# 128 gathered tokens in place of 96 beside the dense experts of a PEER layer, with VectorE alone splitting the second phase's weights

## The chip, the cores and the metric

One core of one Trainium2 chip. The metric is the device time of the whole program in microseconds (us): 3645.8 us is the median of three runs of the kernel before (3645.3 to 3651.99).

## The reference

Two transformer layers, a hybrid mixer and a cross-attention come first; the change does not touch them. It lies in the last layer, PEER: each of 512 tokens chooses 8 x 16 = 128 of 16384 experts by product keys, and the result is a gated sum over them.

```
q = (t @ wq).reshape(ntok, 8, 2, 128)
sc = einsum('thpd,hpkd->thpk', q, subkeys)
s1, i1 = top_k(sc[:, :, 0], 16); s2, i2 = top_k(sc[:, :, 1], 16)
cand = (s1[..., :, None] + s2[..., None, :]).reshape(ntok, 8, 256)
best, pos = top_k(cand, 16)
idx = i1[pos // 16] * 128 + i2[pos % 16]
gate = softmax(best)
act = gelu(einsum('phkd,pd->phk', u_tab[idx], tb)) * gate
out = einsum('phk,phkd->pd', act, v_tab[idx])
```

## The kernel before, in words

**Dense part.** Most tokens are not gathered: for them all 16384 experts are computed. The experts are 128 tiles of 128. In the first phase (steps i = 0 to 127, `up`, L3099) TensorE multiplies the u tile by 416 tokens, ScalarE applies gelu (L3230) and stores the tile to DRAM (`store`, L3202). In the second phase (L3154) the activations come back, are multiplied by gates that are zero for the experts a token did not choose (`gated`, L3450), and are multiplied by the v tile into eight accumulators in PSUM.

**Weights in two parts.** To keep fp32 precision each weight tile is split: SyncE loads it to RAW (L266, three buffers), ScalarE copies it rounded to fp32r (L275), VectorE subtracts the rounded part from the tile (L284, four buffers of both parts), and TensorE makes three matmuls for each of 8 slices (L317 to L319; L3160 to L3162), 24 in a step. For tiles 5 to 67 of the first phase POOL does half of the subtraction (L290; `self.pooled`). ScalarE and VectorE work two or three tiles ahead of TensorE.

**Choice.** Scores (L3102) and top-16 lists (`choice`, L3327) are made on VectorE, for four blocks of 128 tokens in the order 3, 0, 1, 2, in 38 pieces each that are dealt out over the steps (`pieces_by`, L2993). ScalarE makes the exponentials (L3244); `share` (L3370) divides.

**Gates.** From step 70 on a gate tile is built for 8 tokens in each step: one-hot rows of the first index times the gate (L3387) and of the second index (L3390 on VectorE for the first four tokens, L3506 on POOL for the others), multiplied on TensorE (L3136). ScalarE evicts 128x1024 values (L3213) into one of two halves of a buffer; after 64 tokens (a fill) the half is written to DRAM (L3071, L3262). There are seven fills, one of 32 tokens (steps 70 to 73) and six of 64 (from step 74, eight steps each). In the second phase each step reads a gate tile of 416 tokens (L3065).

**Gathered part.** The other 96 tokens (rows 32 to 127 of block 3, 64 and 32 of them) are laid out so that 96 gathers of 128 rows of u serve them: POOL issues an indirect DMA for one row in each partition (L3494), VectorE takes the product and its sum (`dot`, L3408). 46 dots stand at steps 21 to 66 with five buffers, 50 at 77 to 126 with three. In the second phase 96 gathers of v rows with eight buffers, and `sum_` (L3416) adds the scaled rows.

**Order.** Each engine follows one program, written by hand. An engine stops at a wait and everything behind it on that engine stops too. On VectorE a step is: subtraction for tile i + 2, dots, pieces of the choice, one-hots; in the second phase: subtraction, gated, remainder (`rest`, L3455), sums. On ScalarE: weight copy for tile i + 3, gelu, store, evictions, writes of gates.

Of the kernel before, what the change touches and what calls it, by code (L numbers as in the profile page):

```python
# [86 lines left out]
def program(nc, A, out, known, seen):  # L87
# [5 lines left out]
    with ctx:  # L93
# [41 lines left out]
        Gd = nc.dram_tensor("gates_dram", (128, 128, 416), F, kind="Internal").ap()  # L135
        Ad = nc.dram_tensor("acts_dram", (128, 128, 416), F, kind="Internal").ap()
# [16 lines left out]
        g_last = [sem(f"g_last{i}") for i in range(8)]  # L153
        few_in = sem("few_in")
# [22 lines left out]
        T2 = 512  # L177
# [2767 lines left out]
        TD, FEW, HALVES = 416, 96, 64  # L2945
        xtm, few_ = qb(place(1024), 1024), qb(place(192), 192)
        few_i = qb(place(64), 64).bitcast(U32)
        few3 = few_.rearrange("p (i s) -> p i s", i=3)
        spare = UF[:, 0:16 * T2].rearrange("p (k c) -> p k c", c=T2)
        xtm4, four3 = spare[:, :, 416:480], spare[:, 0:3, 480:512]  # L2950
        few = [[few_[:, 64 * i:64 * i + 64] for i in range(3)], [spare[:, i, 480:512] for i in range(3)]]
        few_index = [few_i, spare[:, 3, 480:512].bitcast(U32)]
        gu = [qb(oOn, 1024), qb(oOn + 1024, 1024)] + [qb(oGb + 13312 + 1024 * i, 1024) for i in range(3)]
        gu2 = [CH[:, 1024 * i:1024 * i + 1024] for i in range(3)]
        gv_ = [qb(oGb + 1024 * i, 1024) for i in range(8)]
        few_y = [qb(oGb + 8192, 1024), qb(oGb + 13824, 1024)]
# [8 lines left out]
        ggate = [qb(oOn + 2048 + i * 512, 512) for i in range(4)]  # L2965
        Y = [qb(oY + i * 512, 512) for i in range(4)]
        Gb = [MQ[:, oGb + 8192 * i:oGb + 8192 * i + 8192].rearrange("p (n t) -> p n t", t=64) for i in range(2)]
        scs = [qb(oGb + i * 2048, 2048) for i in range(4)]
# [19 lines left out]
        ORDER = [3, 0, 1, 2]  # L2988
        HERE = 46
        FILLS = [(3, 384, 4)] + [(g // 2, 64 * g, 8) for g in range(6)]  # L2990
        FILL_AT = [70] + [74 + 8 * g for g in range(6)]

        def pieces_by(i):  # L2993
            return 38 * i / 14 if i < 14 else 38 + 114 * (i - 14) / 54

        def exp_at(i):
            return [n for c, n in enumerate(ORDER) if i == 18 * c + 15]

        def share_at(i):
            return [n for c, n in enumerate(ORDER) if i == 18 * c + 16]  # L3000

        def turn_at(i):
            return [n for c, n in enumerate(ORDER) if i == 18 * c + 18]

        def dots_at(i):
            return [s_ for s_ in range(FEW) if i == dot_at(s_)]

        def dot_at(s_):
            return 21 + 45 * s_ // (HERE - 1) if s_ < HERE else 77 + 49 * (s_ - HERE) // (FEW - 1 - HERE)

        def rows(s_):

            return (gu[s_ % 5], gu_in[s_ % 5], s_ // 5 + 1) if s_ < HERE else (
                gu2[s_ % 3], gu_in[5 + s_ % 3], (s_ - HERE) // 3 + 1)

        def gathers_at(i):
            return [s_ for s_ in range(FEW) if i == (
                (18 if s_ < 5 else dot_at(s_ - 5) + 1) if s_ < HERE else (75 if s_ < HERE + 3 else dot_at(s_ - 3) + 1))]

        def sums_at(i):  # L3020
            return [s_ for s_ in range(FEW) if i == 6 + 114 * s_ // 95]

        def group(s_):

            return (0, s_) if s_ < HALVES else (1, s_ - HALVES)
# [11 lines left out]
        def out_sp(i):  # L3037
            return [(f, c) for f in range(7) for c in range(8) if i == last_at(f) + 5 + 3 * c // 4]

        def out_act(i):  # L3040
            return [(f, c) for f in range(7) for c in range(8, 16) if i == last_at(f) + 1 + 3 * (c - 8) // 4]

        def half_of(f):
            return (f + 1) % 2

        def gates_out(f, c):
            lo, m = FILLS[f][1], 8 * FILLS[f][2]
            return (Gd[8 * c:8 * c + 8, :, lo:lo + m].rearrange("n p t -> p n t"), Gb[half_of(f)][:, 8 * c:8 * c + 8, 0:m])

        def peer_sp(e):  # L3050
            def back(j):
# [4 lines left out]
                if j == 0:  # L3056
                    e.wait_ge(g_out[0], 16 * 48)
                if j % 8 == 0 and j < 64:
                    e.wait_ge(g_last[j // 8], 16)
                elif j == 64:  # L3060
                    e.wait_ge(g_out[1], 16 * 56)
# [3 lines left out]
                e.dma_start(ggate[j % 4][:, 0:TD], Gd[j]).then_inc(ga_in[j % 4], 16)  # L3065

            for i in range(NB + 4):
                W.sp(e, iU + i)
                for f, c in out_sp(i):
                    e.wait_ge(S.sem, S.at("gates", f, FILLS[f][2] - 1))  # L3070
                    e.dma_start(*gates_out(f, c)).then_inc(g_last[c] if f == 6 else g_out[half_of(f)], 16)  # L3071
# [6 lines left out]
        def peer_pe(e):  # L3078
# [46 lines left out]
            def gates(n, t8):  # L3125
# [54 lines left out]
        def peer_act(e):  # L3180
# [25 lines left out]
            def evict(n, t8):  # L3206
# [8 lines left out]
                ps.give(S, "gates", n, t8)  # L3215

# [6 lines left out]
            for i in range(NB):  # L3223
# [40 lines left out]
            e.wait_ge(V.sem, V.at("dot", FEW - 1))  # L3264
            for a, _, _ in few:
                e.activation(a, a, ACT.Gelu_apprx_tanh).then_inc(S.sem, S.tick("few"))

            for i in range(NB):
                W.act(e, iD + i + 2)
                if i + 1 < NB:  # L3270
                    rounded(i + 1)
            for d in range(8):
# [4 lines left out]
        def peer_dve(e):  # L3277
# [102 lines left out]
            def one_hots(n, t8):  # L3380
                for half in range(2):
                    i4 = four_at(n, t8) + half
                    a, o, t0 = onA[i4 % 4], onB[i4 % 4], FILLS[n][1] + 8 * t8 + 4 * half
                    if i4 >= 4:
                        e.wait_ge(T.sem, T.at("on", i4 - 4))
                    for i in range(4):
                        e.tensor_scalar(a[:, 128 * i:128 * i + 128], iota, E1[:, t0 + i:t0 + i + 1], Gt[:, t0 + i:t0 + i + 1],  # L3387
                                        ALU.is_equal, MUL).then_inc(V.sem, V.tick("onA", i4))
                    if i4 % 2 == 0:
                        e.tensor_tensor(o.rearrange("p (t n) -> p t n", t=4), iota.unsqueeze(1).to_broadcast([128, 4, 128]),  # L3390
                                        E2[:, t0:t0 + 4].unsqueeze(2).to_broadcast([128, 4, 128]), ALU.is_equal).then_inc(
                                            V.sem, V.tick("onA", i4))

            def indices():

                e.wait_ge(V.sem, V.at("chosen", 3))
                three = CH[:, 1152:1536].rearrange("p (i s) -> p i s", i=3)
                e.tensor_copy(few3[64:128], three[64:128, :, 64:128]).then_inc(V.sem, V.tick())
                e.tensor_copy(four3[32:64], three[32:64, :, 32:64]).then_inc(V.sem, V.tick())
                e.wait_ge(few_in, 16 * 8)  # L3400
# [365 lines left out]
```

## Time and profile before

| | us |
|---|---|
| median of 3 runs | 3645.8 |
| the profiled execution | 3639.07 |
| its span, first to last instruction | 3637.2 |
| TensorE busy in it | 3538.1 |
| VectorE, ScalarE, POOL busy | 2284.6, 1472.4, 884.6 |

The first phase lies at 2356 to 3042 us of the span, the second at 3044 to 3622 us. PE is TensorE, PEld its weight loads, DVE VectorE, ACT ScalarE, SP SyncE. A busy share is an average over a stretch; which engine sets the pace is read from who waits for whom. Matmuls overlap, so their duration (some 350 ns) is longer than their distance; the distance is a stretch's time divided by its number of matmuls.

### The profile page before, as it was taken

To read this page: it belongs to the slowest core of one execution; us is meant where nothing else is said; L and a number is where in the kernel's file an instruction comes from. 1 tells how busy PE (TensorE), PEld (TensorE's weight loads), DVE (VectorE), ACT (ScalarE), POOL (GpSimd) and SP (SyncE) were. 2 spreads that over 40 slices of the span, in tenths; PEclk is the share of its full clock that TensorE was granted. 3 is DMA by queue.
4 is the path that set the end of the run, shared out by engine and by line. 5 is a ranking of instruction groups with operands and counts; after the bars stand their busy time and mean duration, and the time that the engine had idled before them with its cause. 6 is when DMAs were issued, how large, how long until landed. Compare 5 with 4: busy or idle time off the path is not lost.

```text
span 3637.2 us, 56094 instructions
## 1 busy us (share of the span) xinstructions
PE 3538.1 (97%) x22572; PEld 3247.0 (89%) x22572; DVE 2284.6 (63%) x3965; ACT 1472.4 (40%) x2191; POOL 884.6 (24%) x795
## 2 busy tenths in 40 slices
PE   8999999999899999999998999999999999999998
PEld 8988999999797678788677877899999999999998
DVE  7445465554844545555687444479988885777775
ACT  7254453222625435222466444243333433333333
POOL 4010022111401012211213201035646662111110
PEclk9999999999999999999999999999999999999999
DMA  4212232222221123222222122348869999999894
GB/s 155 70 42 65 76 116 93 93 92 94 70 65 54 63 82 133 95 97 93 75 81 70 60 93 81 95 140 272 281 214 258 298 289 338 314 310 313 307 312 139
DMA packets 293617, 544.70 MB, mean 150 GB/s; under 512 B 138288, under 2 KB 187568, under 8 KB 292976
## 3 DMA queue, kind: packets, MB, share of 16 engines
q1 hardware_dynamic: 185248, 394.34, 32.6%
q0 software_dynamic: 27648, 100.68, 8.4%
q10 hardware_dynamic: 80464, 46.10, 4.3%
q8 instruction: 180, 2.95, 0.3%
q14 instruction: 77, 0.63, 0.0%
HBM read 483.67 MB, written 56.62 MB: 149 GB/s over the span
## 4 chain that ended last, share of the span: by engine, by line
PE 86%; DVE 8%; ACT 3%; issue 1%; POOL 1%; DMA 0%; ACTq 0%; DVEq 0%; POOLq 0%
PE PSM L317 19%; PE PSM L318 18%; PE PSM L319 18%; PE PSM L211 5%; PE PSM L3160 5%; PE PSM L3162 5%; PE PSM L3161 5%; PE PSM L3136 3%; DVE PARTS L284 2%; ACT PARTS L275 1%; PE PSM L1061 1%; DVE MH L1741 1%; PE PSM L825 1%; PE PSM L1097 1%; DVE QK L1375 1%
## 5 line engine op out<-in xcount | busy, mean ns | idle before, releaser
L284 DVE TENSOR_TENSOR PARTS<-RAW,PARTS 128x1024 fp32r<-128x1024 f32 (+1 forms) x612 | 743.8, 1220 | 476.4 <-ACT PARTS L275 476.2
L275 ACT ACTIVATE PARTS<-RAW 128x1024 fp32r<-128x1024 f32 x612 | 645.4, 1057 | 932.1 <-PE PSM L319 488.6
L317 PE MATMUL PSM<-UX,PARTS 128*128 128x264 f32 (+3 forms) x2912 | 987.1, 339 | 27.4 <-DVE UX L2297 4.9
L318 PE MATMUL PSM<-UX,PARTS 128*128 128x264 f32 (+3 forms) x2912 | 970.2, 333 | 0.0
L319 PE MATMUL PSM<-UX,PARTS 128*128 128x264 f32 (+3 forms) x2912 | 969.5, 333 | 0.0
L317 PEld LDWEIGHTS PSM<-UX,PARTS 128*128 128x128 f32 x2912 | 548.8, 188 | 78.4 <-issue 9.2
L318 PEld LDWEIGHTS PSM<-UX,PARTS 128*128 128x128 f32 x2912 | 549.0, 189 | 29.9 <-issue 1.7
L319 PEld LDWEIGHTS PSM<-UX,PARTS 128*128 128x128 f32 x2912 | 547.9, 188 | 29.7
L3160 PE MATMUL PSM<-AC,PARTS 128*128 128x416 f32 x1024 | 358.3, 350 | 2.3 <-DVE AC L3457 2.3
L3162 PE MATMUL PSM<-AC,PARTS 128*128 128x416 f32 x1024 | 357.6, 349 | 0.0
L3161 PE MATMUL PSM<-AC,PARTS 128*128 128x416 f32 x1024 | 357.5, 349 | 0.0
L317 PE MATMUL PSM<-HD,PARTS 128*128 128x264 f32 (+1 forms) x992 | 315.3, 318 | 15.0 <-DVE XL L600 13.1
L319 PE MATMUL PSM<-HD,PARTS 128*128 128x264 f32 (+1 forms) x992 | 314.8, 317 | 0.0
L318 PE MATMUL PSM<-HD,PARTS 128*128 128x264 f32 (+1 forms) x768 | 247.3, 322 | 0.0
L1679 POOL TENSOR_TENSOR FT<-FT 128x528 f32<-128x528 f32 (+1 forms) x56 | 108.3, 1935 | 458.2 <-DVE FT L1708 458.2
L317 PEld LDWEIGHTS PSM<-HD,PARTS 128*128 128x128 f32 x992 | 187.4, 189 | 29.5 <-DVE XL L600 14.1
L319 PEld LDWEIGHTS PSM<-HD,PARTS 128*128 128x128 f32 x992 | 187.3, 189 | 13.2
L3160 PEld LDWEIGHTS PSM<-AC,PARTS 128*128 128x128 f32 x1024 | 192.4, 188 | 2.9 <-ACT MQ L3230 2.6
L3161 PEld LDWEIGHTS PSM<-AC,PARTS 128*128 128x128 f32 x1024 | 192.4, 188 | 0.3
L3162 PEld LDWEIGHTS PSM<-AC,PARTS 128*128 128x128 f32 x1024 | 192.3, 188 | 0.4
L3230 ACT ACTIVATE MQ<-PSM 128x416 f32<-128x416 f32 x128 | 66.1, 517 | 293.6 <-PE PSM L319 293.6
L3506 POOL TENSOR_SCALAR MQ<-MH,MQ 128x128 f32<-128x128 f32 x208 | 171.0, 834 | 52.5 <-PE PSM L3136 28.5
(516 smaller groups left out, 5815.9 us busy)
## 6 DMA issues: line engine op xcount, KB each, us to landing
RAW<-w_ff_dram SPq DMA_DIRECT2D x128, 512.0 KB, 3.2
RAW<-peer_u_dram SPq DMA_DIRECT2D x128, 512.0 KB, 4.8
RAW<-peer_v_dram SPq DMA_DIRECT2D x128, 512.0 KB, 5.1
RAW<-w_in_dram SPq DMA_DIRECT2D x116, 512.0 KB, 3.2
acts_dram<-MQ ACTq DMA_DIRECT2D x128, 208.0 KB, 4.2
MQ<-acts_dram SPq DMA_DIRECT2D x128, 208.0 KB, 3.8
MQ<-gates_dram SPq DMA_DIRECT2D x128, 208.0 KB, 4.7
RAW<-w_mix_o_dram SPq DMA_DIRECT2D x32, 512.0 KB, 3.3
```

The costliest lines, as they stand in the source:

```text
L211: m = e.matmul(PSM[0:rows, b + s, 0:hi - lo], lhs[k], rhs[k][:, lo:hi], start=(k == 0), stop=(k == len(lhs) - 1))
L275: e.activation(p[:, 0:1024], self.raw.of(i), ACT.Copy).then_inc(S.sem, S.tick("w", i))
L284: e.tensor_tensor(p[:, 1024:1024 + n], r[:, 0:n], p[:, 0:n].bitcast(F), SUB).then_inc(V.sem, V.tick("w", i))
L317: e.matmul(dst, wh[k], xh_[k][:, lo:hi], start=(k == 0), stop=False, skip_group_check=True)
L318: e.matmul(dst, wh[k], xl_[k][:, lo:hi], start=False, stop=False, skip_group_check=True)
L319: m = e.matmul(dst, wl[k], xh_[k][:, lo:hi], start=False, stop=(k == kk - 1), skip_group_check=True)
L1679: e.tensor_tensor(x, x, x, MUL).then_inc(G.sem, G.tick("relu2", l, i))
L3136: m = e.matmul(PSM[:, b + half, 128 * i:128 * i + 128], a[:, 128 * i:128 * i + 128], o[:, 128 * i:128 * i + 128], start=True, stop=True, s ...
L3160: e.matmul(PSM[:, acc[d], 0:TD], vh[d], ah, start=(i == 0), stop=False, skip_group_check=True)
L3161: e.matmul(PSM[:, acc[d], 0:TD], vh[d], al, start=False, stop=False, skip_group_check=True)
L3162: m = e.matmul(PSM[:, acc[d], 0:TD], vl[d], ah, start=False, stop=(i == NB - 1), skip_group_check=True)
L3506: e.tensor_scalar(o[:, 128 * i:128 * i + 128], iota, E2[:, t0 + i:t0 + i + 1], None, ALU.is_equal).then_inc(G.sem, G.tick("onB", i4))
```

## The change

384 tokens are computed densely and 128 are gathered, which is all of block 3.

- The 32-token fill goes. The layout of the gathered tokens becomes one token for each partition, so the copies between partitions (eight small DMAs) go.
- 108 dots stay in the first phase: 30 at steps 21 to 70, 78 at steps 80 to 126 with three buffers. The last 20 dots and all 128 sums move to one list of 148 items over steps 6 to 122 of the second phase, with seven buffers in a space that the first phase's tokens held. ScalarE's gelu of the 128 dots moves to step 20 of the second phase.
- The choice ends at steps 15, 34, 53 and 72 (before: all four by step 68), and POOL's half of the subtraction reaches to tile 73. The set `pooled` holds no tile of the second phase, so the two places where the second phase asks for it find nothing: VectorE subtracts there alone, and POOL only issues gathers.
- One-hots of the first index for the second four tokens of a step go from VectorE to ScalarE, as relu(1 - |index - i|) in five instructions; they carry no gate, which POOL's one-hots of the second index now multiply in.
- Fills 0 to 3 go to DRAM in runs of 64 x 8 values, and come back for four steps at a time; fills 4 and 5 stay in SBUF, so `gated` becomes two products of 128 and 256 columns.

```diff
-                self.pooled = {first["pu"] + i for i in range(5, 68)}
+                self.pooled = {first["pu"] + i for i in range(5, 74)}
...
-        TD, FEW, HALVES = 416, 96, 64
+        TD, FEW, LATE = 384, 128, 20
...
+        gv_ = [UF[:, 1024 * i:1024 * i + 1024] for i in range(7)]
...
+        ORDER, END = [3, 0, 1, 2], [15, 34, 53, 72]
+        HERE, THERE = 30, FEW - LATE
+        FILLS = [(g // 2, 64 * g, 8) for g in range(6)]
+        FILL_AT = [74 + 8 * g for g in range(6)]
...
+            return 21 + 50 * s_ // (HERE - 1) if s_ < HERE else 80 + 46 * (s_ - HERE) // (THERE - 1 - HERE)
...
+        def late_by(r):
+            return 6 + 116 * r // (FEW + LATE - 1)
...
+        def late_gathers_at(i):
+            return [r for r in range(FEW + LATE) if i == (0 if r < 7 else late_by(r - 7) + 1)]
...
+            return Gd[f, :, 8 * c:8 * c + 8, :], Gb[half_of(f)][:, 8 * c:8 * c + 8, :]
...
+                if j % 4 == 0:
+                    if j >= 8:
+                        e.wait_ge(V.sem, V.at("gated", j - 5))
+                    e.dma_start(ggate[j // 4 % 2].rearrange("p (f m) -> p f m", f=4),
+                                Gd[:, :, j:j + 4, :].rearrange("f p n t -> p f (n t)")).then_inc(gg_in[j // 4 % 2], 16)
...
+            def one_hots(n, t8):
+                i4 = four_at(n, t8) + 1
+                a, t0 = onA[i4 % 4], FILLS[n][1] + 8 * t8 + 4
...
+                for i in range(4):
+                    e.activation(a[:, 128 * i:128 * i + 128], iota, ACT.Abs, bias=E1[:, t0 + i:t0 + i + 1],
+                                 scale=-1.0).then_inc(S.sem, S.tick("off", i4))
+                e.wait_ge(S.sem, S.at("off", i4))
+                e.activation(a, a, ACT.Relu, bias=con["ones"][:, 0:1], scale=-1.0).then_inc(S.sem, S.tick("onA", i4))
...
+                for n, t8 in gates_at(i + 1):
+                    one_hots(n, t8)
                 for n, t8 in gates_at(i):
                     evict(n, t8)
...
+                e.tensor_tensor(y, y, kept[:, i], MUL).then_inc(V.sem, V.tick())
+                e.wait_ge(gg_in[i // 4 % 2], 16 * (i // 8 + 1))
+                e.tensor_tensor(x, x, gate4[i // 4 % 2][:, i % 4], MUL).then_inc(V.sem, V.tick("gated", i))
...
-                    e.tensor_scalar(o[:, 128 * i:128 * i + 128], iota, E2[:, t0 + i:t0 + i + 1], None,
-                                    ALU.is_equal).then_inc(G.sem, G.tick("onB", i4))
+                    e.tensor_scalar(o[:, 128 * i:128 * i + 128], iota, E2[:, t0 + i:t0 + i + 1], Gt[:, t0 + i:t0 + i + 1],
+                                    ALU.is_equal, MUL).then_inc(G.sem, G.tick("onB", i4))
...
+            for i in range(NB):
+                if iD + i + 2 in W.pooled:
+                    W.pool(e, iD + i + 2)
+                for r in late_gathers_at(i):
+                    if r == 0:
+                        e.wait_ge(T.sem, T.at("pu", NB - 1))
+                    if r >= LATE + 7:
+                        e.wait_ge(V.sem, V.at("sum", r - LATE - 7))
+                    elif r >= 7:
+                        e.wait_ge(V.sem, V.at("dot", THERE + r - 7))
```

## Rows read from the trace of the kernel before

**Rows 1.** The page, part 1: busy us (share of the span) xinstructions.

```profile
PE 3538.1 (97%) x22572; PEld 3247.0 (89%) x22572; DVE 2284.6 (63%) x3965; ACT 1472.4 (40%) x2191; POOL 884.6 (24%) x795
```

**Rows 2.** Stretches: us, busy PE, PEld, DVE, ACT, POOL; clock; DMA share; GB/s.

```profile
600.00:900.00 300.00, 300.00 (x2476) 300.00 (x2475) 150.53 (x155) 72.91 (x83) 54.69 (x29) 1.00 0.28 92
1500.00:1750.00 250.00, 250.00 (x1085) 203.76 (x1084) 131.82 (x138) 61.65 (x68) 43.66 (x23) 1.00 0.29 95
...
2460.00:2690.00 230.00, 230.00 (x1225) 228.56 (x1225) 227.09 (x731) 84.56 (x111) 124.55 (x93) 1.00 0.80 270
2700.00:3010.00 310.00, 310.00 (x1984) 309.92 (x1983) 252.72 (x586) 125.05 (x151) 210.03 (x244) 1.00 0.95 274
3030.00:3060.00 30.00, 27.74 (x141) 27.24 (x140) 14.04 (x21) 9.80 (x16) 3.49 (x3) 0.94 1.12 359
3060.00:3100.00 40.00, 40.00 (x216) 39.94 (x215) 27.88 (x35) 13.52 (x19) 13.48 (x10) 1.00 1.02 398
3100.00:3600.00 500.00, 500.00 (x2681) 499.22 (x2680) 356.49 (x426) 168.03 (x224) 77.77 (x83) 1.00 0.87 298
```

**Rows 3.** Waits at 3100 to 3600 us: total, times, longest.

```profile
ACT PARTS L275 <- PE PSM L3162: 333.7, 112, 3.0
```

**Rows 4.** The chain of waits, two gate steps: start, us, what.

```profile
2750.19 1.78 PE PSM L3136 x16
2756.45 1.78 PE PSM L3136 x16
```

**Rows 5.** Waits at 3020 to 3060 us.

```profile
DVE MQ L3453 <- DMA MQ<-gates_dram: 3.7, 3, 2.1
...
PE PSM L3160 <- DVE AC L3457: 2.3, 1, 2.3
```

**Rows 6.** VectorE's groups at 2460 to 2690 us, the dots: xcount | busy, mean ns.

```profile
L3413 DVE SCALAR_TENSOR_TENSOR MQ<-MQ 128x1024 f32<-128x1024 f32 x46 | 55.9, 1216 | 0.0
...
L3413 DVE DVE_READ_ACCUMULATOR MQ<-MQ 128x1 f32 x46 | 3.7, 81 | 0.0
```

**Rows 7.** Groups at 2700 to 3010 us, the gate stage.

```profile
L3506 POOL TENSOR_SCALAR MQ<-MH,MQ 128x128 f32<-128x128 f32 x196 | 159.0, 822 | 29.0 <-PE PSM L3136 28.5
...
L3387 DVE TENSOR_SCALAR MQ<-MH,MQ 128x128 f32<-128x128 f32 x397 | 116.5, 353 | 0.0
...
L275 ACT ACTIVATE PARTS<-RAW 128x1024 fp32r<-128x1024 f32 x50 | 52.6, 1052 | 8.2 <-ACT MQ L3213 4.3 <-issue 3.6
L3213 ACT ACTIVATE MQ<-PSM 128x1024 f32<-128x1024 f32 x50 | 51.2, 1025 | 65.6 <-PE PSM L3136 59.5 <-DVE MQ L3387 2.5 <-issue 2.3
```

**Rows 8.** ScalarE's groups at 2380 to 3640 us.

```profile
L3244 ACT ACT_TABLE_LOAD x4 | 5.1, 1283 | 0.1
...
L3244 ACT ACTIVATE CH<-CH 128x128 f32<-128x128 f32 x4 | 1.2, 311 | 0.4 <-DVE CH L3367 0.4
```

**Rows 9.** ScalarE's queue and POOL in order of time, 2770 to 2784 us.

```profile
2781.56 0.34 ACTq L3204 DMA_DIRECT2D acts_dram<-MQ  x1
...
2770.94 2.60 POOL L3506 TENSOR_SCALAR MQ<-MH,MQ 128x128 f32<-128x128 f32 x4 [0.60 <-PE PSM L3136]
...
2777.21 4.64 POOL L3506 TENSOR_SCALAR MQ<-MH,MQ 128x128 f32<-128x128 f32 x4 [0.32 <-PE PSM L3136]
```

**Rows 10.** The gathers of the gate stage, by groups and by line L3494.

```profile
L3494 POOL DMA_INDIRECT CH<-peer_rows_dram,UF x30 | 31.5, 1049 | 46.9 <-DVE MQ L3387 46.9
...
DMA to landing us min/median/max: 4.3/6.3/9.3
```

**Rows 11.** DMA packets at 2700 to 3010 us.

```profile
DMA packets 121046, 84.98 MB, mean 274 GB/s; under 512 B 102192, under 2 KB 108592, under 8 KB 121020
```

**Rows 12.** VectorE's groups at 3100 to 3600 us, the second phase.

```profile
L284 DVE TENSOR_TENSOR PARTS<-RAW,PARTS 128x1024 fp32r<-128x1024 f32 x112 | 137.2, 1225 | 143.5 <-ACT PARTS L275 143.5
L3429 DVE SCALAR_TENSOR_TENSOR MQ<-MQ 128x1024 f32<-128x1024 f32 x59 | 75.5, 1280 | 0.0
L3453 DVE TENSOR_TENSOR MQ<-MQ 128x416 f32<-128x416 f32 x112 | 65.4, 584 | 0.0
```

More of the change, by code:

```diff
@@ L2944, in program @@
         sm = qb(place(16), 16)
[L2945 to L2952 removed]
+        TD, FEW, LATE = 384, 128, 20
+        xtm = qb(place(1024), 1024)
+        few_a, few_g, few_i = qb(oE1 + TD, 128), qb(oGt + TD, 128), qb(oE2 + TD, 128).bitcast(U32)
         gu = [qb(oOn, 1024), qb(oOn + 1024, 1024)] + [qb(oGb + 13312 + 1024 * i, 1024) for i in range(3)]
         gu2 = [CH[:, 1024 * i:1024 * i + 1024] for i in range(3)]
[L2955 to L2956 removed]
+        gv_ = [UF[:, 1024 * i:1024 * i + 1024] for i in range(7)]
+        few_y = UF[:, 7168:8192]
         assert at[0] <= STAGE - 3072
@@ L2980, in program @@
         iP, iU, iD = first["pq"], first["pu"], first["pd"]
[L2988 to L2991, printed above, removed]
+        ORDER, END = [3, 0, 1, 2], [15, 34, 53, 72]
+        HERE, THERE = 30, FEW - LATE
+        FILLS = [(g // 2, 64 * g, 8) for g in range(6)]
+        FILL_AT = [74 + 8 * g for g in range(6)]
         def pieces_by(i):
-            return 38 * i / 14 if i < 14 else 38 + 114 * (i - 14) / 54
+            c = sum(i >= x for x in END)
+            if c == 4:
+                return 38 * 4
+            lo = END[c - 1] if c else 1
+            return 38 * c + 38 * (i - lo) / (END[c] - lo)
@@ L3016, in gathers_at @@
-        def gathers_at(i):
[L3017 to L3025, printed above, removed]
+            if s_ < HERE:
+                return gu[s_ % 5], gu_in[s_ % 5], s_ // 5 + 1
+            return gu2[s_ % 3], gu_in[5 + s_ % 3], (s_ - HERE) // 3 + 1
@@ new lines, in late, with late_at @@
+        def late(r):
+            return gv_[r % 7], gv_in[r % 7], r // 7 + 1
+        def gathers_at(i):
+            return [s_ for s_ in range(THERE) if i == (
+                (18 if s_ < 5 else dot_at(s_ - 5) + 1) if s_ < HERE else (77 if s_ < HERE + 3 else dot_at(s_ - 3) + 1))]
+        def late_by(r):
+            return 6 + 116 * r // (FEW + LATE - 1)
+        WHOLE = late_by(LATE)
+        def late_at(i):
+            return [r for r in range(FEW + LATE) if i == late_by(r)]
+        def late_gathers_at(i):
+            return [r for r in range(FEW + LATE) if i == (0 if r < 7 else late_by(r - 7) + 1)]
@@ L3056, in back @@
                 if j == 0:
[L3057 to L3061, printed above, removed]
+                    for out_ in g_out:
+                        e.wait_ge(out_, 16 * 32)
                 if j >= 4:
@@ L3271, in peer_act @@
                     rounded(i + 1)
+                if i == WHOLE - 1:
+                    e.wait_ge(V.sem, V.at("dot", FEW - 1))
+                    e.activation(few_a, few_a, ACT.Gelu_apprx_tanh).then_inc(S.sem, S.tick("few"))
             for d in range(8):
@@ L3380, in one_hots @@
             def one_hots(n, t8):
[L3381 to L3392, printed above, removed]
+                i4 = four_at(n, t8)
@@ L3408, in dot @@
             def dot(s_):
-                x, landed, turn_ = rows(s_)
-                w, c = group(s_)
+                x, landed, turn_ = rows(s_) if s_ < THERE else late(s_ - THERE)
                 e.wait_ge(landed, 16 * turn_)
-                xv = x.rearrange("p (k c) -> p k c", c=64) if w else x
-                e.scalar_tensor_tensor(out=xv, in0=xv, scalar=1.0, in1=xtm4 if w else xtm, op0=MUL, op1=MUL,
-                                       accum_out=few[w][0][:, c:c + 1]).then_inc(V.sem, V.tick("dot", s_))
+                if s_ == 0:
+                    e.wait_ge(S.sem, S.at("xtm"))
@@ L3416, in sum_ @@
+                e.scalar_tensor_tensor(out=x, in0=x, scalar=1.0, in1=xtm, op0=MUL, op1=MUL,
+                                       accum_out=few_a[:, s_:s_ + 1]).then_inc(V.sem, V.tick("dot", s_))
             def sum_(s_):
-                w, c = group(s_)
-                x, a, y = gv_[s_ % 8], few[w][0][:, c:c + 1], few_y[w]
-                e.wait_ge(gv_in[s_ % 8], 16 * (s_ // 8 + 1))
+                x, landed, turn_ = late(LATE + s_)
+                a = few_a[:, s_:s_ + 1]
+                e.wait_ge(landed, 16 * turn_)
@@ L3528, in peer_pool @@
                     one_hots(n, t8)
-            e.wait_ge(g_out[0], 16 * 48)
-            for s_ in range(FEW):
-                if s_ >= 8:
-                    e.wait_ge(V.sem, V.at("sum", s_ - 8))
-                else:
-                    e.wait_ge(V.sem, V.at("al", s_ + 1))
-                gather(gv_[s_ % 8], A["peer_v"].rearrange("n p d -> (n p) d"), s_, gv_in[s_ % 8])
+            for i in range(NB):
[8 more added lines that the diff above has]
+                        e.wait_ge(V.sem, V.at("dot", THERE + r - 7))
+                    to, landed, _ = late(r)
+                    if r < LATE:
+                        gather(to, A["peer_rows"], THERE + r, landed)
+                    else:
+                        gather(to, A["peer_v"].rearrange("n p d -> (n p) d"), r - LATE, landed)
             for p in range(3):
```

121 lines of the change are left out of this document (53 added, 68 removed).

## The prediction

> **What bounds the kernel now.** I read the page first: PE is busy 3538.1 of 3637.2 us [rows 1]. A matmul's busy time overlaps its neighbours', so I went to the table of stretches next and counted matmuls per us. In the second phase (3100 to 3600 us) 2681 matmuls of 416 columns take 500 us, 186.5 ns each, and weight loads fill 499.22 us [rows 2]: PE runs back to back. The waits of that stretch say the same from the other side: ACT waited 112 times, 2.98 us each, for PE to hand a weight buffer back [rows 3]. VectorE is busy 356.49 of 500 us, the DMA engines 0.87 [rows 2]. In the first phase PE is busy for all of the choice (2460 to 2690) and all of the gate stretch (2700 to 3010), with VectorE at 227.09 of 230 and 252.72 of 310 [rows 2]. The chain of waits shows a gate step: two gate products start 6.26 us apart and take 1.78 [rows 4], which leaves 4.48 for the 24 weight matmuls. So TensorE sets the pace of all 256 steps, and the change must be judged by the columns that it takes away and by whether anything else can keep the shorter step.
>
> **Columns.** Dense tokens go from 416 to 384, in 2 x 128 x 24 = 6144 matmuls. No row has 384 columns. The rows beside it: 264 columns 300/2476 = 121.2 ns, 416 columns 186.5, 512 columns 250/1085 = 230.4 [rows 2]. Between 264 and 416 a column costs 0.430 ns, between 416 and 512 0.457; 32 columns are 13.75 to 14.6 ns. I take 13.75, since 384 lies in the first interval: **-84.5 us** (bound -89.8). A step becomes 24 x 172.7 ns = 4.15 us, a gate step 4.15 + 1.78 = 5.93.
>
> **Gate steps.** The fill of 32 tokens at steps 70 to 73 goes; 48 gate steps stay of 52. Four times 1.78 us [rows 4]: **-7.1 us**.
>
> **Between the phases.** PE waited 2.3 us once for the first gated activations, and these for a gate tile's DMA, 3.7 us in all [rows 5], because the last fill was written to DRAM and read back. Now fills 4 and 5 stay in SBUF and the first gate quad can be read long before. PE still waits for the last gelu (0.5 us): **-2 us**; bounds 0, if something else is late there, and -4, as the granted clock was only 0.94 in 3030 to 3060 and may not fall [rows 2]. The constants before the first gather, eight small transfers and their waits, go too; PE did not wait for them, so nothing.
>
> **Choice stage.** Dots here fall from 46 to 30, each 1.216 + 0.081 us [rows 6], 20.8 us of VectorE's work, and the choice is spread over 4 more steps. VectorE's 227 us become 206 plus 3 for four more weight halves, in 51 steps x 4.15 + 16.6 = 228 us: 92%. Cover is there, and it is thinner only at the three 2048-element operations that end each block. Nothing, bound +6.
>
> **Gate stage, engine by engine, against 5.93 us.**
> VectorE loses four of its eight one-hot products (353 ns each, [rows 7]) and gains dots: 78 dots in 47 steps, 1.66 a step. Now 252.72/49.5 steps = 5.1 us; minus 4 x 0.27 (that is 353 less the overlap) plus 0.66 x 1.30 gives 4.9.
> ACT takes the four products over: four Abs of 128x128, for which the nearest row is an exponential of 128x128, 311 ns [rows 8], and a Relu of 512 columns, which I put between 0.52 and 0.65 us (below a 1024-column eviction's 1.025, [rows 7]). With the copy of the weights 1.05 and the eviction 1.03 [rows 7], a gelu of 384 columns between the two (0.5) and 1.67 transfers to issue at 0.34 [rows 9] this is 1.9 + 3.2 = 5.1 us. The one-hots stand ahead of the eviction on ACT, and the next weight copy behind it, so VectorE's step starts about 1 us later than now. No row shows Abs. If it needed a table of its own, two loads of 1.283 us [rows 8] would come to each gate step: ACT at 7.7, 1.8 us over, 48 x 1.8 = +86. The Trainium skill (ScalarE: Activation LUTs, Table sets: the hidden batching unit) says that relu and abs are in every set; no run here shows it, and without that sentence I would still hold it unlikely, since copies and gelus alternate here without a load.
> POOL multiplies the gate into its one-hots: the same four instructions with a second operation. Now 0.822 us each [rows 7], four of them between 2.60 and 4.64 us [rows 9]. With 1.66 gathers of 1.049 [rows 10] POOL is at 3.3 + 1.7 = 5.0 us. The price of the second operation is not in the trace: from nothing to a doubling (1.64 us). I take 0 to 0.2, since the long and the short times of one and the same instruction show that most of it is not arithmetic.
> DMA: gates are written in 2 KB runs for four fills in place of 256 B runs for seven; under 512 B were 102192 of 121046 packets in this stage [rows 11]. Per step 0.52 MB of weights, 0.87 of gathers, 0.20 of activations, 0.52 of gates: 2.1 MB in 5.93 us, 357 GB/s, against 274 now at a share of 0.95 [rows 2].
> What is tight is the **gather loop**: three buffers, 1.66 dots a step. In one step out of three a gather is issued in the step of its own dot: dot, POOL's issue, landing (4.3, median 6.3, at most 9.3 us, [rows 10]), dot, one-hots, PE. From the dot that frees the buffer to PE's need of the one-hots there are about 5.93 + 4.1 = 10 us; 6.3 + 1.3 + 1.7 = 9.3 fits, 9.3 + 3.0 = 12.3 does not. Some 16 such steps, I charge 0.6 us each: **+10 us** (0 to 37).
>
> **Second phase against 4.15 us.** VectorE alone subtracts the rounded weights, as it does now: no item of this kernel's second phase moves to or from POOL. What grows is the sums: 148 dots and sums in 117 steps, 1.265 each. From 584 ns for 416 columns and 1225 for 1024 [rows 12] a column is 1.054 ns and the fixed part 146: the two gated products of 128 and 256 columns 0.28 + 0.42, the remainder of 384 columns 0.55. Sum 1.225 + 0.70 + 0.55 + 1.265 x 1.28 = 4.09 us without any overlap. A step now is by the same rows 1.225 + 2 x 0.584 + 0.83 x 1.28 = 3.46 us, where the stretch has VectorE busy for 356.49 us in 2681/24 = 111.7 steps, 3.19 each [rows 2]: instructions overlap to 0.92, so 3.77 us. It holds, with 9% to spare, and two buffers' lead (weights are split two steps ahead) evens out steps with two sums. If a gather lands late, the next subtraction is queued behind the sum that waits for it; with seven buffers a gather has some 4.5 steps, 18 us, for a landing of 5 to 9.
> DMA per step: 0.524 weights, 1.265 x 0.524 gathers, 0.197 activations, 0.131 gates: 1.515 MB, 365 GB/s, against 298 now. The highest sustained row is 398 GB/s at 3060 to 3100, with PE at its full rate (216 matmuls in 40 us, [rows 2]). So it fits, at 92%. **0 us** (to +33).
> The Trainium skill (DMA: Bandwidth & Descriptors, Specifications) gives about 358 GB/s of HBM for one core; by it the step is estimated at 4.23 us and this phase 10 us longer. The 398 of the row is above that figure, and the row decides.
>
> **Sum.** -84.5 - 7.1 - 2 + 10 = -84; a further stall of about 1 us where the gates begin (exponential, share and the first one-hots in one step) is as it is now. The profiled execution's 3639.1 (span 3637.2) becomes 3555; it lies 6.7 below the median of 3645.8, to which I apply the same difference: **3562 us**. VectorE, POOL and ACT only lose cover; what becomes late next is the gather loop in the gate stage.
>
> **Rivals.**
> A, the gather loop bounds the gate stage: three dots per 1.3 + 3.3 (POOL in its one-hots) + 6.3 + 1.1 = 12 us means 6.65 us a step, +0.72 x 47 = 34 in place of 10: 3586. For it: landing times to 9.3 and POOL busy in order. Against: DMA's small packets vanish. Chance 0.16.
> B, the second phase becomes DMA-bound: 1.515 MB at 359 GB/s (row 3030 to 3060, share 1.12) is 4.22 us, at 298/0.87 = 343 GB/s 4.42; 117 steps x 0.07 to 0.27 = +8 to +32: 3570 to 3594. Against: the 398 row. Chance 0.13. The Trainium skill's 358 GB/s, above, would land in this case.
> C, nothing stalls: 3552 or, with 14.6 ns, 3547. Chance 0.14, part of the forecast's neighbourhood.
> D, slower: POOL's one-hots with two operations cost twice, 1.64 us. Then POOL needs 4 x 1.64 + 1.7 = 8.3 us in each of 48 gate steps, PE waits 2.4, +114: 3552 + 114 = 3666. It decides from 1.54 us an instruction, where 48 steps of 4 x 1.54 + 1.74 give the 94 us back. For it: collisions already bring four to 4.64 us. Chance 0.07. With ACT's table loads (3638) 0.02.
> E, VectorE is over the second phase's step because chained sums cannot overlap: 4.3 us, +18: 3580. Chance 0.05.
> That the change does not do what it says: POOL's weights end at step 73 of the first phase, so it can't take one in the second; no chance given.
>
> **How the numbers follow.** The forecast with small stalls has 0.43. The range holds C, the forecast, A and B's most: 3545 to 3598; D and the sum of A and B are left out. A measurement of this kernel tells some 0.2%, 7 us: faster 0.91, same 0.02 (table loads and a mild D), slower 0.07 (D).
>
> **What would show it.** Right: second phase with 172 to 174 ns between matmuls and PE without idle time, VectorE near 3.8 us a step, DMA near 365 GB/s; gate steps 5.93 with a few longer, whose wait is on VectorE behind a gather. Wrong: PE waiting on POOL's one-hots (D), on ACT's, or in the second phase on VectorE while that waits for a gather (B) or for nothing (E).

## The result and the profile after

The changed kernel takes 3630.7 us at the median (3647.6 before, on the same chips): ratio 0.9947, 95% interval 0.9935 to 0.9959. It is faster, by 0.5% where 2.3% were forecast; 3562 us missed by 69, and the range ended at 3598. The profiled execution took 3626.0 us, span 3624.2. Two disturbed executions, of 6894 us here and of 4817 us in the run without dots below, count in no median.

The table of stretches (us, busy PE, PEld, DVE, ACT, POOL; clock; DMA share; GB/s), which answers to [rows 2]:

```profile
3100.00:3600.00 500.00, 500.00 (x2886) 500.00 (x2886) 441.54 (x647) 176.03 (x240) 189.56 (x141) 1.00 0.95 348
2460.00:2690.00 230.00, 225.68 (x1304) 224.74 (x1303) 225.44 (x695) 92.57 (x126) 119.38 (x81) 1.00 0.72 235
2700.00:3010.00 310.00, 260.99 (x1620) 254.75 (x1619) 196.64 (x366) 175.27 (x324) 278.57 (x224) 0.94 0.77 256
```

The second phase is as forecast: 500/2886 = 173.3 ns from one matmul to the next, PE without a gap. The loss is all in the third line. PE is busy for 261 of 310 us and POOL for 279, where it was 210 [rows 2]. From the starts of the weight matmuls, steps 78 to 120 of the first phase are 7.58 us apart on the mean, with single ones up to 13.4; 5.93 were forecast, and 6.27 were measured before. From the start of step 78 to that of step 120 are 42 such distances: 42 x 1.65 = 69 us, as much as the miss.

The line numbers below are those of the changed kernel: L3511 is POOL's one-hots (before: L3506), L3499 its gathers (L3494), L3420 the dots (L3413), L3400 and L3402 VectorE's one-hots of the first and of the second index (L3387, L3390), L283 its subtraction (L284), L3147 the gate products (L3136). In the experiments they shift by some lines.

The groups of that stage, 2720 to 3000 us, as in [rows 7, 10] (xcount | busy, mean ns of one | idle time before):

```profile
L3511 POOL TENSOR_SCALAR MQ<-MH,MQ 128x128 f32<-128x128 f32 x146 | 179.1, 1233 | 2.8 <-PE PSM L3147 1.4
L3499 POOL DMA_INDIRECT CH<-peer_rows_dram,MQ x59 | 77.4, 1312 | 21.8 <-DVE MQ L3400 11.0 <-issue 7.9 <-DVE CH L3420 1.6
...
L3420 DVE SCALAR_TENSOR_TENSOR CH<-CH,MQ 128x1024 f32<-128x1024 f32 x60 | 74.0, 1242 | 69.8 <-DMA CH<-peer_rows_dram,MQ 69.6
L3400 DVE TENSOR_SCALAR MQ<-MH,MQ 128x128 f32<-128x128 f32 x140 | 47.1, 420 | 0.0
L283 DVE TENSOR_TENSOR PARTS<-RAW,PARTS 128x1024 fp32r<-128x1024 f32 x36 | 44.5, 1236 | 25.8 <-ACT PARTS L274 25.8
```

and the waits there (total, times, longest):

```profile
DVE CH L3420 <- DMA CH<-peer_rows_dram,MQ: 69.6, 25, 7.0
...
PE PSM L3147 <- DVE MQ L3402: 28.0, 11, 5.6
PE PSM L3147 <- POOL MQ L3511: 10.0, 7, 2.5
```

POOL's one-hot takes 1.23 us in place of 0.82, its gather 1.31 in place of 1.05. Yet the longest waits name VectorE, behind a dot that waits for a landing. Read by those rows alone, the gather loop would be the cause.

PE's waits there come to 43 of 280 us, but the stage has lost 60: 280 us hold 37 steps, each 1.63 us over the undisturbed 5.95. The other 17 us are time in which PE is busy longer for the same matmuls. The granted clock is 0.95 on the mean from 2720 to 3000 us, where it was 1.00 before, and 280 us at 0.95 lack 14 us of full clock. It fell after PE had stood (columns as in [rows 2]):

```profile
2885.00:2890.00 5.00, 1.36 (x8) 1.04 (x6) 1.08 (x1) 2.38 (x6) 2.70 (x4) 0.90 0.97 344
2890.00:2895.00 5.00, 3.06 (x14) 3.08 (x15) 5.00 (x13) 0.00 (x0) 4.53 (x3) 0.50 0.69 190
```

0.50 is the lower of the two levels, 1.2 in place of 2.4 GHz. So a wait of PE cost more here than its own length.

The order of time shows why POOL's instruction is long. POOL first, then VectorE (start, us, what):

```profile
2849.66 6.24 POOL L3511 TENSOR_SCALAR MQ<-MH,MQ 128x128 f32<-128x128 f32 x4
...
2859.38 3.13 POOL L3511 TENSOR_SCALAR MQ<-MH,MQ 128x128 f32<-128x128 f32 x4
```

```profile
2848.95 1.53 DVE L283 TENSOR_TENSOR PARTS<-RAW,PARTS 128x1024 fp32r<-128x1024 f32 x1 [1.98 <-ACT PARTS L274]
2850.40 1.21 DVE L3420 SCALAR_TENSOR_TENSOR CH<-CH,MQ 128x1024 f32<-128x1024 f32 x1
2851.54 0.08 DVE L3420 DVE_READ_ACCUMULATOR CH<-CH,MQ 128x1 f32 x1
2851.54 1.22 DVE L3420 SCALAR_TENSOR_TENSOR CH<-CH,MQ 128x1024 f32<-128x1024 f32 x1
2852.69 0.08 DVE L3420 DVE_READ_ACCUMULATOR CH<-CH,MQ 128x1 f32 x1
2852.69 1.16 DVE L3400 TENSOR_SCALAR MQ<-MH,MQ 128x128 f32<-128x128 f32 x4
2853.77 0.68 DVE L3402 TENSOR_TENSOR MQ<-MH,MQ 128x512 f32<-128x512 f32 x1
...
2863.59 1.23 DVE L3420 SCALAR_TENSOR_TENSOR CH<-CH,MQ 128x1024 f32<-128x1024 f32 x1 [5.23 <-DMA CH<-peer_rows_dram,MQ]
```

At 2859.38 VectorE waits for a landing, and four one-hots take 3.13 us, 0.78 each. At 2849.66 VectorE is in a run of three instructions without a gap that each read two tensors from SBUF; the run ends at 2852.77. The first of POOL's four, by itself:

```profile
2849.66 3.61 POOL L3511 TENSOR_SCALAR MQ<-MH,MQ 128x128 f32<-128x128 f32 x1
```

It takes 2.8 us more than one alone and ends 0.5 us after the run: POOL stood until the run was over. VectorE's one-hots after it (L3400, one tensor) cost POOL's second 0.07 us (0.86), the comparison L3402 (two tensors) its third 0.22 (1.01). Of the 46 one-hots of POOL at 2720 to 3000 us that started with more than 0.4 us of such a run left, 42 ended 0.50 to 0.68 us after its end; four ended before it. All of POOL's one-hots there, sorted by what VectorE did meanwhile (an overlap of over 10 ns counts):

```
POOL's one-hots, mean ns (count)     before (1 operation)   after (2 operations)
VectorE idle                          600 (34)               792 (57)
only one-tensor instructions beside   658 (78)               none
a two-tensor instruction beside      1130 (68)              1517 (88)
```

The Trainium skill (SBUF — State Buffer, Who interferes with whom) has this as a rule: a VectorE instruction with two SBUF inputs and a GpSimd (POOL) instruction that reads SBUF use the same port, and the one that starts later is blocked until the other ends. The rows agree that one blocks the other. They show that POOL mostly stood not only for the instruction that was running when it came, but for the run of them. That the resource is a port is the page's statement; the runs show the blocking.

### The profile page after: what moved, and what is told of

It reads as the page before. It is cut to its first block, busy times and chain, and to the rows that moved or that the text cites. A ratio compares the mean times of both kernels' runs of the same rounds, so it can differ in the third digit from the quotient of the medians.

```text
span 3624.2 us, 56046 instructions
## 1 busy us (share of the span) xinstructions
PE 3468.8 (96%) x22489; PEld 3173.6 (88%) x22489; DVE 2311.8 (64%) x3955; ACT 1548.5 (43%) x2424; POOL 1096.1 (30%) x849
## 4 chain that ended last, share of the span: by engine, by line
PE 77%; DVE 10%; POOL 5%; ACT 3%; DMA 3%; issue 2%; ACTq 0%; DVEq 0%; POOLq 0%
PE PSM L316 17%; PE PSM L317 16%; PE PSM L318 16%; PE PSM L210 5%; PE PSM L3173 5%; PE PSM L3174 5%; PE PSM L3175 5%; POOL MQ L3511 3%; DMA CH<-peer_rows_dram,MQ 3%; DVE PARTS L283 2%; ACT PARTS L274 1%; POOL CH L3499 1%; DVE CH L3420 1%; PE PSM L1060 1%; DVE MH L1740 1%
## 5 line engine op out<-in xcount | busy, mean ns | idle before, releaser
L316 PE MATMUL PSM<-UX,PARTS 128*128 128x264 f32 (+3 forms) x2912 | 978.0, 336 | 29.5 <-DVE UX L2296 4.9
L283 DVE TENSOR_TENSOR PARTS<-RAW,PARTS 128x1024 fp32r<-128x1024 f32 (+1 forms) x612 | 743.5, 1220 | 358.4 <-ACT PARTS L274 358.1
L317 PE MATMUL PSM<-UX,PARTS 128*128 128x264 f32 (+3 forms) x2912 | 960.3, 330 | 0.0
L318 PE MATMUL PSM<-UX,PARTS 128*128 128x264 f32 (+3 forms) x2912 | 959.3, 329 | 0.0
L3173 PE MATMUL PSM<-AC,PARTS 128*128 128x384 f32 x1024 | 343.0, 335 | 0.9 <-ACT MQ L3248 0.9
L3174 PE MATMUL PSM<-AC,PARTS 128*128 128x384 f32 x1024 | 342.4, 334 | 0.0
L3175 PE MATMUL PSM<-AC,PARTS 128*128 128x384 f32 x1024 | 342.3, 334 | 0.0
L3499 POOL DMA_INDIRECT UF<-peer_v_dram,MQ x128 | 174.8, 1366 | 245.4 <-DVE UF L3432 217.0
L3511 POOL TENSOR_SCALAR MQ<-MH,MQ 128x128 f32<-128x128 f32 x192 | 231.7, 1213 | 17.6 <-DVE CH L3381 14.5
```

Of the source, the lines that this page charges most:

```text
L283: e.tensor_tensor(p[:, 1024:1024 + n], r[:, 0:n], p[:, 0:n].bitcast(F), SUB).then_inc(V.sem, V.tick("w", i))
L316: e.matmul(dst, wh[k], xh_[k][:, lo:hi], start=(k == 0), stop=False, skip_group_check=True)
L317: e.matmul(dst, wh[k], xl_[k][:, lo:hi], start=False, stop=False, skip_group_check=True)
L318: m = e.matmul(dst, wl[k], xh_[k][:, lo:hi], start=False, stop=(k == kk - 1), skip_group_check=True)
L3173: e.matmul(PSM[:, acc[d], 0:TD], vh[d], ah, start=(i == 0), stop=False, skip_group_check=True)
L3174: e.matmul(PSM[:, acc[d], 0:TD], vh[d], al, start=False, stop=False, skip_group_check=True)
```

## The experiments

Time is a kernel's median, the ratio is to the kernel before; "steps" is the mean distance of steps 78 to 120, read as above. Edits are shortened to what matters. Two theories stood first: POOL's own work bounds the gate stage, or the loop of three gather buffers does.

**POOL compares only.**

```diff
-  e.tensor_scalar(o[...], iota, E2[...], Gt[...], ALU.is_equal, MUL)
+  e.tensor_scalar(o[...], iota, E2[...], None, ALU.is_equal)
```

> POOL's one-hots of the gate stage go back to one operation (the comparison alone); the gates of the second four tokens of each step are left out. The changed kernel takes 3631 us and its 48 gate steps average 7.5 us where 5.93 were forecast. Theory 1 (POOL is the bound: four one-hots at 1.22 us and 1.7 gathers at 1.34 fill its step): with 0.82 us an instruction POOL needs 3.3 + 2.3 = 5.6 us, gate steps fall to 6.0 to 6.4 and the time to 3565 to 3585. Theory 2 (the loop of three gather buffers, dot to issue to landing to dot, is the bound): the loop loses only the 1.6 us that POOL's one-hots are shorter in the steps where a gather is issued behind them, steps stay at 7.0 to 7.4, time 3610 to 3625.

3593.6 us, ratio 0.9847 (0.9830 to 0.9865), steps 6.76: 37 us faster than the changed kernel, half of what was missing. Theory 2's range is left by far, theory 1's missed by 9 us: its 0.82 us for one comparison did not hold either, as the group shows.

```profile
L3511 POOL TENSOR_SCALAR MQ<-MH,MQ 128x128 f32<-128x128 f32 x163 | 158.6, 985 | 3.1 <-PE PSM L3147 1.8
```

**No gathers.**

```diff
+  if s_ >= HERE + 3: continue        # POOL's gathers of the gate stage
-  e.wait_ge(landed, 16 * turn_)      # the dot
+  e.wait_ge(V.sem, V.at("dot", s_ - 3))
```

> The 75 gathers of the gate stage from the fourth on are left out, and with them the waits of the dots for their landing; the 75 dots still run, on rows that are not theirs. Theory 1: POOL has only its one-hots, 4 x 1.22 = 4.9 us, below 5.93, so steps fall to 5.93 to 6.1 and the time to 3555 to 3568. Theory 2: the loop is gone, the same 3555 to 3568. A third theory (VectorE beside it stretches POOL's four one-hots to some 6 us whether it gathers or not): steps stay at 6.2 to 6.6, time 3573 to 3592.

3557.2 us, 0.9752 (0.9736 to 0.9768), steps 5.95. So nothing but POOL, its gathers and their transfers stands between the changed kernel and the forecast; the first two theories had the same range and are not told apart. The third theory fell on the time, but its mechanism is in the group: with VectorE never stopped for a landing, a one-hot of POOL takes 1.47 us, and four fill 5.9 of a 5.95 us step.

```profile
L3514 POOL TENSOR_SCALAR MQ<-MH,MQ 128x128 f32<-128x128 f32 x173 | 252.8, 1474 | 2.7 <-PE PSM L3147 2.7
```

**No dots.** VectorE's 78 dots of the gate stage are left out; a gather waits for the landing of the third before it.

```diff
-  dot(s_)
+  if s_ < HERE: dot(s_)
-  e.wait_ge(V.sem, V.at("dot", s_ - 3))                      # POOL, before a gather
+  e.wait_ge(rows(s_ - 3)[1], 16 * rows(s_ - 3)[2])
```

> The gathers of the gate stage stay, but its 78 dots are left out; each gather waits only for the landing of the one three before it. Theory 1 (POOL's own work): POOL still has 4 x 1.22 + 1.7 x 1.34 = 7.2 us of work in a step, steps 6.8 to 7.4, time 3600 to 3627. Theory 2 (the loop): no dot and no late landing stands ahead of VectorE's one-hots, steps 5.93 to 6.1, time 3555 to 3568. In between (6.2 to 6.7, 3573 to 3597) if POOL's instructions are 1.22 us only because VectorE works beside them: VectorE loses 1.7 x 1.24 = 2.1 us of each step.

3574.7 us, 0.9805 (0.9785 to 0.9824), steps 6.43: the middle case. POOL has as many instructions in a step as in the changed kernel, but its one-hots are shorter, with VectorE busy for 128.9 of 280 us in place of 179.3.

```profile
L3514 POOL TENSOR_SCALAR MQ<-MH,MQ 128x128 f32<-128x128 f32 x168 | 177.1, 1061 | 3.0 <-PE PSM L3147 1.4
```

**POOL in the second phase.**

```diff
-  self.pooled = {first["pu"] + i for i in range(5, 74)}
+  self.pooled = {first["pu"] + i for i in range(5, 74)} | {first["pd"] + i for i in range(8, 120)}
```

> The second phase's remainders of the weights are halved between VectorE and POOL, as in the first phase; the rest is the changed kernel. The forecast's own step (the second phase is TensorE's at 4.16 us, VectorE at 3.67 has room): no change, 3624 to 3638. A rival (VectorE is near its limit there and saves time with half of the subtraction gone): would be faster by up to 10 us, but PE shows no idle time to win. The other rival (POOL, with 1.37 us gathers and four subtractions of some 0.9 us each, delays gathers or VectorE): slower, 3640 to 3670.

3666.1 us, 1.0059 (1.0040 to 1.0078): 35 us slower than the changed kernel, as the other rival said; with POOL's half, the whole change would be no gain. The kernel before leaves this work to VectorE as well, so here the change keeps something; it is no source of its gain. PE is busy for 469.5 of 500 us at 3100 to 3600, where the changed kernel has it busy for all. Groups of VectorE at 3100 to 3500 us:

```profile
L3432 DVE SCALAR_TENSOR_TENSOR UF<-UF,MQ 128x1024 f32<-128x1024 f32 x92 | 165.7, 1802 | 2.0
L283 DVE TENSOR_TENSOR PARTS<-RAW,PARTS 128x512 fp32r<-128x512 f32 x89 | 73.8, 829 | 1.3 <-ACT PARTS L274 1.3
L3464 DVE TENSOR_TENSOR AC<-MQ,AC 128x384 fp32r<-128x384 f32 x88 | 70.1, 796 | 0.0
L3458 DVE TENSOR_TENSOR MQ<-MQ 128x128 f32<-128x128 f32 x89 | 59.9, 673 | 0.3 <-DMA MQ<-acts_dram 0.3
```

In the changed kernel the same sums take 1.281 us, the remainders 0.553 and the products of 128 columns 0.285. POOL takes 512 columns off a 1.22 us instruction, and what VectorE saves, some 0.4 us, it pays back with some 1.1 us in longer instructions: here POOL holds up VectorE.

**The gate on ScalarE**, all outputs kept, POOL comparing only:

```diff
-  e.activation(a, a, ACT.Relu, bias=ones, scale=-1.0)
+  for i in range(4):
+      e.activation(x_i, x_i, ACT.Relu, bias=Gt[...], scale=NG[...])     # NG = -Gt
...
-  e.tensor_scalar(o[...], iota, E2[...], Gt[...], ALU.is_equal, MUL)    # POOL
+  e.tensor_scalar(o[...], iota, E2[...], None, ALU.is_equal)
```

> The gate of the second four tokens moves from POOL's one-hots to ScalarE's: Relu with scale -gate and bias gate, four of 128 columns in place of one of 512, and POOL compares only. Nothing is left out. ScalarE had 3.85 us of work in a 5.95 us step where no gather stood in the way, and gets some 0.85 more. Theory 1 (POOL's own work, lengthened while VectorE works): as with the comparison alone, 3588 to 3600. If ScalarE's later one-hots became the wait: 3605 to 3630.

3593.2 us, 0.9856 (0.9840 to 0.9873), steps 6.81, as theory 1 said. ScalarE had the room: busy for 215.7 of 280 us.

**Wide one-hots on POOL.**

```diff
-  4 x e.tensor_scalar(o_i, iota, E2[...], None, ALU.is_equal)
+  e.tensor_tensor(o4, iota4, E2 broadcast, SUB); e.tensor_scalar(o, o, 0.0, None, ALU.is_equal)
```

> As the run before it (gate on ScalarE), and POOL makes its four one-hots in two instructions of 512 columns (a subtraction of the token's number, a comparison with zero) in place of four of 128. Theory 1: POOL has 1.3 to 1.6 us for the subtraction, about 1.2 for the comparison, and 1.7 gathers of 1.4: 5.0 us, some 1.2 less than with four comparisons; steps 6.0 to 6.3, time 3565 to 3582. Theory 2 (three gather buffers bound what is left): 3585 to 3597. A rival: a two-input subtraction on POOL lengthens VectorE's instructions, as in the second phase where POOL subtracted; then VectorE is late, 3595 to 3620.

3594.9 us, 0.9864 (0.9848 to 0.9881), steps 6.83: no gain over four comparisons. The time lies where theory 2 and the rival's lower end meet, and VectorE's groups speak for the rival: dots of 1.56 us in place of 1.25. But POOL's comparison also took 2.13 us where about 1.2 were expected, so the run does not tell the two apart.

```profile
L3524 POOL TENSOR_SCALAR MQ<-MQ 128x512 f32<-128x512 f32 x41 | 87.2, 2126 | 3.6
L3520 POOL TENSOR_TENSOR MQ<-MH,MQ 128x512 f32<-128x512 f32 x41 | 45.5, 1109 | 2.3 <-PE PSM L3148 1.0 <-issue 0.3
...
L3429 DVE SCALAR_TENSOR_TENSOR CH<-CH,MQ 128x1024 f32<-128x1024 f32 x67 | 103.8, 1564 | 25.3 <-DMA CH<-peer_rows_dram,MQ 25.2
```

**Five gather buffers**, nothing else:

```diff
-  gu2 = [CH[:, 1024 * i:1024 * i + 1024] for i in range(3)]
+  gu2 = [... the same three] + [UF[:, 16 * TD + 1024 * i:16 * TD + 1024 * i + 1024] for i in range(2)]
```

> The changed kernel with five buffers for the gate stage's gathers in place of three (the halves of the activations are packed to 384 columns, which leaves 2048 columns for two more). Theory 1 (POOL): a gather may be issued earlier, but POOL's work is the same 7.1 us a step, steps 7.0 to 7.4, time 3608 to 3630. Theory 2 (the loop of three buffers): VectorE's waits for a landing, 77 us in the gate stage, go; steps 6.0 to 6.3, time 3560 to 3580.

3640.7 us (seven executions, 3624.8 to 3644.0), 0.9965 (0.9945 to 0.9985), steps 7.81. No gain is shown, and theory 2 alone falls: VectorE never waits for a landing, POOL is busy for 264 of 280 us, and PE waits for POOL. Theory 1 has the mechanism, but its range, up to 3630, was missed by 11 us, since it held POOL's work in a step to be the same.

```profile
L3515 POOL TENSOR_SCALAR MQ<-MH,MQ 128x128 f32<-128x128 f32 x142 | 206.2, 1460 | 2.5 <-PE PSM L3149 1.2
...
PE PSM L3149 <- POOL MQ L3515: 36.8, 24, 2.3
```

Taking VectorE's wait away lengthened POOL's one-hots, from 1.23 to 1.46 us. So those waits were time in which POOL caught up.

**Gate on ScalarE and five buffers**, the edits of both runs:

> Both: the gate on ScalarE and five buffers. Theory 1 and 2 together (POOL needs 6.2 us a step, the loop is out of the way): steps 6.1 to 6.4, time 3566 to 3582. If theory 1 alone held, no gain over the gate on ScalarE: 3588 to 3600. If theory 2 alone held, no gain over five buffers.

3572.3 us, 0.9798 (0.9782 to 0.9814), steps 6.41: both together, as expected. Buffers help only once POOL is lighter.

**VectorE compares all eight**, on top of it:

```diff
-  e.tensor_tensor(o[512 columns], iota x 4, E2[:, t0:t0 + 4] broadcast, ALU.is_equal)
+  e.tensor_tensor(o[1024 columns], iota x 8, E2[:, t0:t0 + 8] broadcast, ALU.is_equal)
...
-  for n, t8 in gates_at(i): one_hots(n, t8)     # POOL
```

> The gate on ScalarE and five buffers, as in the fastest run so far (3572 us), and VectorE compares all eight tokens of a step in one instruction of 1024 columns (512 before), so that POOL only gathers. Nothing is left out. If POOL's instructions are the bound because VectorE's two-input instructions hold them up, POOL is off the path: it has 1.7 gathers of 1.0 to 1.4 us. VectorE gains 1.22 - 0.68 = 0.54 us a step and stands at 5.4 of 5.95. Steps 5.95, time 3555 to 3566. Rival: VectorE becomes the bound in the steps with two dots, 3572 to 3590.

3556.8 us, 0.9745 (0.9727 to 0.9764): the fastest, and every step of 78 to 120 is 5.95 us, with all gathers and their transfers in place. The stretch 2700 to 3000:

```profile
2700.00:3000.00 300.00, 300.00 (x2004) 299.96 (x2003) 255.06 (x444) 253.52 (x528) 122.90 (x78) 1.00 0.90 322
```

**The same with three buffers.**

```diff
-  return gu2[(s_ - HERE) % 5], ...
+  return gu2[s_ % 3], ...
```

> As the run with all eight comparisons on VectorE, with the changed kernel's three buffers in place of five. If the loop of three buffers was long only by what stood on POOL ahead of a gather: three dots, an issue at once and a landing of 4 to 6 us fit into 1.8 steps, 3556 to 3568, as with five. If three buffers are too few by themselves: VectorE waits for landings, 3573 to 3592.

3571.1 us, 0.9782 (0.9762 to 0.9802), steps 6.34. Between the two cases: three buffers by themselves cost 14 us.

**One-tensor comparisons on VectorE**, in the changed kernel:

```diff
-  e.tensor_tensor(o, iota x 4, E2 broadcast, ALU.is_equal)
+  4 x e.tensor_scalar(o_i, iota, E2[...], None, ALU.is_equal)
```

> The changed kernel, but VectorE makes its four comparisons in four instructions of 128 columns with one tensor as input (0.38 us each) in place of one of 512 columns with two (0.68 us). VectorE works 0.85 us longer in each step. Theory a (only VectorE's two-input instructions hold POOL up): POOL's one-hots, 1.22 us on the mean, get shorter, 1.0 to 1.15, and the time is 3605 to 3632. Theory b (any work of VectorE does): they get longer, 1.25 to 1.4, and the time is 3640 to 3670.

3614.3 us, 0.9904 (0.9885 to 0.9924), steps 7.20: faster with more work on VectorE, as theory a has it and theory b does not. Its number for POOL's one-hots was missed: 1.20 us, barely below 1.23; the gathers fell further, from 1.31 to 1.20. VectorE also waited less for landings (55 us in place of 70), which after the run with five buffers should lengthen POOL's one-hots again; that is argued, not shown.

**VectorE's one-hots before its dots**, in the changed kernel (all gate steps but the first):

```diff
+  for n, t8 in gates_at(i): one_hots(n, t8)
   for s_ in dots_at(i): dot(s_)
-  for n, t8 in gates_at(i): one_hots(n, t8)
```

> The changed kernel with one thing in VectorE's order: in a gate step its one-hots come before the dots, not behind them, so that no landing stands ahead of what TensorE needs. Order theory (the gate steps are long since VectorE's one-hots are queued behind a dot that waits for its gather; TensorE waited 28 us for them at 2720 to 3000 us): that wait goes, steps 6.2 to 6.8, time 3575 to 3605. POOL theory (TensorE's wait for VectorE only takes the place of a wait for POOL): POOL's four comparisons and its gathers still take 7 us or more of a step, TensorE waits for POOL instead, steps 7.1 to 7.7, time 3612 to 3645.

3633.4 us, 0.9966 (0.9955 to 0.9977), steps 7.71. The order theory falls: PE now waits for POOL.

```profile
PE PSM L3147 <- POOL MQ L3516: 37.4, 13, 4.5
```

## Why the prediction was wrong by 69 us

- **Columns, gate steps, between the phases.** Right. A step is 4.16 us (4.15 forecast), 48 gate steps stay, and PE's wait for the first activations fell from 2.3 us to 0.9. With POOL's one-hots gone and five buffers the kernel takes 3557 us; the forecast's sum without stalls (rival C) was 3552.
- **Choice stage.** Right in effect. VectorE is at 98% (225.44 of 230 us), not 92%; two steps were 0.8 and 1.0 us longer, within the bound of 6.
- **Second phase.** Right: 4.16 us a step, VectorE 441.54/120.2 = 3.67 us (3.77), DMA 364 GB/s from 3100 to 3500 us (365). Rivals B and E did not occur. The Trainium skill's 358 GB/s for a core (DMA: Bandwidth & Descriptors, Specifications) would have meant 4.23 us; the measured rate is above it.
- **ScalarE.** Abs took 0.388 us (0.311 assumed), the Relu 0.723 (0.52 to 0.65), with no table load of their own. PE waited for these one-hots for 4.8 us of its 43 at 2720 to 3000 us; the time in which ScalarE had them done was not what bound the stage, as the run with the gate on ScalarE shows, which gives it more work and is faster.
- **The failed step: POOL's share of the gate step, "POOL is at 3.3 + 1.7 = 5.0 us", and the 0.9 us of slack that it left for the second operation.** The operation's own price was rightly put ("I take 0 to 0.2"): alone it costs 0.19 us (0.600 to 0.792). The sum put it at nothing, as if it fell into slack; taking it away gave 0.82 us a step and half of the miss. For the other half, 0.822 was the mean over an interplay: the same instruction took 0.65 or 1.16 in [rows 9] according to what VectorE did. I carried the mean over to a step that is shorter and has 1.66 dots in place of one. POOL was busy for 255.4 us in 280, 6.9 us of each 7.58 us step: about 4 x 1.23 and 1.6 x 1.31, where 5.93 were to be kept.
- **Gather loop, +10 (0 to 37).** By itself 14 us (five against three buffers with POOL free). In the changed kernel it looked like 70, because a gather is queued behind up to 6.2 us of POOL's one-hots.
- **Rival D** had the engine right, with a chance of 0.07, and the reason wrong: it let the second operation double the instruction. It asked for 1.64 us an instruction and lost the gain from 1.54; measured were 1.23 with VectorE often stopped, and 1.47 where it ran freely. Its "collisions already bring four to 4.64 us" was the row to follow: I named it and did not ask what VectorE did in those 4.64 us.

## What to carry to other kernels

Before moving work between VectorE and POOL, sort one POOL instruction of the trace by what VectorE does beside it, and price it at its slow value if VectorE is to fill up. A wait that disappears from VectorE can come back as time on POOL, so look at how full POOL is (255 of 280 us here), not only at the longest wait. In this kernel, with VectorE nearly full of two-tensor instructions, it paid to leave POOL its gathers and to widen one VectorE instruction (512 to 1024 columns, 0.68 to 1.22 us) rather than run four beside it on POOL.

## What was not expected of the hardware

- POOL's 128x128 one-hot mostly stands until an unbroken run of VectorE's two-tensor instructions is over (42 of 46 in the changed kernel; 13 of 22 in the kernel before): up to 3.79 us for 0.79 us of work.
- It goes the other way too: sums of 1.28 us on VectorE took 1.80, and a 0.285 us product 0.67, beside POOL's subtractions.
- A 512-column comparison with a constant on POOL took 2.13 us on the mean and 1.49 at the least; two 128-column ones of the run before it took 2.01.
- POOL's gather instruction varied from 0.93 to 2.73 us in one stage. The 16 that met an idle VectorE took at most 1.03 us, the 43 beside a two-tensor instruction 1.43 on the mean; but in the kernel before all 43 ran beside one and took 1.02 to 1.11. What lengthens it was not tried by itself.
